# Encoder layer on eight cores: the mixer's output projection in seven products instead of eight, with casts, statistics and first loads re-queued

## The reference

```python
h = rms_norm(x, g_mix)
q, k, v, cu, cb, cc, gl = split(h @ w_in)        # 8 q heads, 2 k/v heads of 128; conv width 1024
y_attn = windowed_gqa_sink(rope(q), rope(k), v, sink) @ w_attn_out
y_conv = (cb * short_conv_centred(cc * cu, conv_w)) @ w_conv_out
g_a, g_c = split(sigmoid(gl + b_gate))
x = x + (g_a * y_attn + g_c * y_conv) @ w_o      # the output projection of this case
x = x + memory_cross_attention(rms_norm(x, g_cross), rms_norm(mem, g_mem), w_cq, w_ckv, w_co)
hf = rms_norm(x, g_ffn)
x = x + (silu(hf @ w_gate) * (hf @ w_up)) @ w_down
return rms_norm(x, g_final)
```

## Time and profile before

| | |
|---|---|
| median of 3 runs | 3403.1 us (3401.38 to 3403.25) |
| the profiled execution | 3398.95 us |
| its span (slowest core, 2) | 3397.9 us; all cores 3389.7 to 3397.9 us |
| TensorE busy | 3264.5 us (96%) |
| VectorE, ScalarE, GpSimd busy | 1916.3, 927.4, 858.1 us |
| DMA | 315.34 MB |
| granted TensorE clock, mean | 0.991 |
| chain that ended last | 90% TensorE, 4% VectorE, 2% issue |

### The profile page before, as it was taken

The page is one execution under the profiler, slowest core; times in us unless marked ns, Lnnn a source line. Parts: engine busy times, 40 slices in busy tenths (PEclk is TensorE's granted clock), DMA queues, the critical chain, the costliest instruction groups (busy, mean ns, idle before and its releaser), DMA issues.

```text
span 3397.9 us, 48543 instructions; the slowest of 8 cores (3389.7 to 3397.9 us)
## 1 busy us (share of the span) xinstructions
PE 3264.5 (96%) x15813; PEld 1534.5 (45%) x16118; DVE 1916.3 (56%) x3109; ACT 927.4 (27%) x1790; POOL 858.1 (25%) x1001
## 2 busy tenths in 40 slices
PE   5899999999899999999999999999989999999997
PEld 3455444444344444444454444444434444444445
DVE  4855644526755454635687655553386454554465
ACT  4355221135411010101453532112361011111115
POOL 1311122221222231312463112222221222222233
PEclk8999999999999999999999999999999999999999
DMA  8434544573346555545685335557333545454545
GB/s 203 77 69 75 87 82 87 91 164 56 62 70 99 75 86 87 83 80 91 132 184 118 62 56 92 85 85 177 64 60 60 90 76 96 69 98 74 96 73 139
DMA packets 117029, 315.34 MB, mean 93 GB/s; under 512 B 13488, under 2 KB 22064, under 8 KB 116784
## 3 DMA queue, kind: packets, MB, share of 16 engines
q0 software_dynamic: 81216, 256.02, 45.8%
q1 hardware_dynamic: 35568, 56.19, 5.8%
HBM read 551.36 MB, written 16.78 MB: 167 GB/s over the span
## 4 chain that ended last, share of the span: by engine, by line
PE 90%; DVE 4%; issue 2%; ACT 1%; DMA 1%; POOL 0%; SPq 0%; DVEq 0%; ACTq 0%; POOLq 0%
PE ps L333 89%; DVE arena L351 3%; ACT arena L348 1%; PE ps L336 1%; DMA arena<-xT 1%; POOL arena L351 0%; SPq L374 0%; DMA arena<-wp 0%; DVE arena L355 0%; DVE arena L362 0%; DVE arena L359 0%; DVEq L144 0%; DVE arena L368 0%; ACTq L144 0%; ACT ps L348 0%
## 5 line engine op out<-in xcount | busy, mean ns | idle before, releaser
L333 PE MATMUL ps<-arena 128*128 128x512 bf16 (+2 forms) x15317 | 3241.8, 370 | 120.7 <-DVE arena L351 53.4
L333 PEld LDWEIGHTS ps<-arena 128*128 128x128 bf16 x15622 | 1505.7, 98 | 1840.8 <-issue 166.2
L351 DVE TENSOR_TENSOR arena<-ps,arena 128x512 f32<-128x512 f32 (+4 forms) x1542 | 982.2, 660 | 1271.2 <-PE ps L333 1231.2
L348 ACT ACTIVATE arena<-arena 128x512 f32<-128x512 f32 (+8 forms) x1128 | 646.9, 620 | 1045.2 <-DVE arena L351 437.1
L351 DVE TENSOR_TENSOR arena<-arena 128x1024 bf16<-128x1024 bf16 (+5 forms) x1192 | 755.4, 669 | 125.4 <-ACT arena L348 56.3
L351 POOL TENSOR_TENSOR arena<-arena 128x512 f32<-128x512 f32 (+2 forms) x433 | 556.9, 1294 | 959.5 <-DVE arena L351 792.9
L374 POOL DMA_DIRECT2D arena<-wp x560 | 303.9, 544 | 1572.7 <-PE ps L333 1361.4
L348 ACT ACTIVATE arena<-ps 128x512 f32<-128x512 f32 (+3 forms) x332 | 212.5, 654 | 1234.1 <-PE ps L333 925.3
L348 ACT ACTIVATE arena<-ps,arena 128x256 f32<-128x256 f32 (+4 forms) x123 | 61.4, 516 | 124.6 <-PE ps L333 93.4
L359 DVE SCALAR_TENSOR_TENSOR arena<-arena 128x1024 f32<-128x1024 f32 (+1 forms) x48 | 67.8, 1428 | 23.5 <-ACT arena L348 21.6
L355 DVE TENSOR_SCALAR arena<-arena 128x4 f32<-128x4 f32 (+3 forms) x145 | 44.5, 341 | 33.5 <-DMA arena<-xT 26.7
(11 more groups left out here) (8 smaller groups left out, 6.1 us busy)
## 6 DMA issues: line engine op xcount, KB each, us to landing
arena<-wp POOLq DMA_DIRECT2D x400, 512.0 KB, 5.7
arena<-xT SPq DMA_DIRECT2D x128, 256.0 KB, 13.8
arena<-wp POOLq DMA_DIRECT2D x96, 256.0 KB, 4.2
arena<-wp POOLq DMA_DIRECT2D x64, 320.0 KB, 5.4
outT<-arena SPq DMA_DIRECT2D x48, 256.0 KB, 4.1
outT<-arena SPq DMA_DIRECT2D x32, 128.0 KB, 3.0
arena<-cs SPq DMA_DIRECT2D x4, 576.0 KB, 10.8
arena<-memT SPq DMA_DIRECT2D x16, 128.0 KB, 8.7
```

The lines of the kernel that those rows point to most:

```text
L333: pr.add("pe", lambda e: e.matmul(out, lhsT, rhs, start=start, stop=stop), reads=[lhsT, rhs], writes=[out])
L348: pr.add("act", lambda e: e.activation(out, in_, func, **kw), reads=rd, writes=wr)
L351: pr.add(eng, lambda e: e.tensor_tensor(out, in0, in1, op), reads=[in0, in1], writes=[out])
```

## The change

Six edits:

1. `out_proj` goes in pairs of weight pieces, 7 products of 8 matmuls each for 2 column chunks x 2 halves. The products are added to x in place: c1 is copied by ScalarE, u and e1 are made by VectorE, three sums (x21+u, x12+e1, x22+e1) by GpSimd, five by VectorE. Half 0's statistics are all on VectorE, half 1's all on GpSimd, with a ring of two slots. Only half 0 is cast here.
2. Token sums of `mT` (`merged_sums`, `outT`) are made in the second half of `mix`, the last behind `gated(15)`, and `pair_sums` of the first pair ahead of it.
3. Half 1 is cast in `cross`, steps t = 2 and 3.
4. `post` is split: casts first, squares and their adds later; the four banks `bs` are taken one by one; the merges for two `finish` calls are emitted earlier, and in `first_blocks` `finish` itself one block earlier.
5. `qkv_first`: V's weight loads wait for chunks 7 and 11 of x instead of 9 and 13, the cos and sin tables are loaded in the middle of the second half of x, `k_ropes(0)` comes behind all casts, and two q projections stand ahead of the halo's `finish`.
6. The 32 final chunks of tile 0: VectorE's half of them read 1/rms from a bank.

```diff
@@ generate
+    outT = chunks8([kv_lo, kv_lo + 4352, kv_lo + 6400, kv_lo + 10240, kv_lo + 14848, q_lo + 32768, c_lo + 8192, rstd_lo]
+                   + [rstd_lo + 1024 * i for i in (1, 2, 3)] + [acc_lo + 2048, acc_lo + 3072]
+                   + [h_lo + 16384 + 1024 * i for i in (8, 9, 10)] + [h_lo + 16384 + 1024 * i for i in range(8)])
+    accO = view(h_lo + 16384 + 11264, F32, (2, HW))
@@ qkv_first
-        wissue(xT[:, 0, 9, :]); wissue(xT[:, 0, 13, :])
-        load_cs(0, xT[:, 0, 13, :])
+        wissue(xT[:, 0, 7, :]); wissue(xT[:, 0, 11, :])
         for c in range(16):
             dma_x(xT[:, 1, c, :], c, HW, HW)
+            if c == 9:
+                load_cs(0)
...
-        casts(0, 6)
+        casts(0, 12)
         half_scales(0, st0)
-        casts(6, 11)
+        v_out(vb)
+        casts(12, 16)
+        ring.flush()
         k_ropes(bk, 0)
-        v_out(vb)
-        casts(11, 16)
-        ring.flush()
...
-        b = proj2(wF(("in", 0)), hk)
-        wfree()
+        qb = []
+        for h in range(2):
+            qb.append(proj2(wF(("in", h)), hk))
+            wfree()
+            for hf in range(2):
+                q_rope(qb[h][hf], h, hf)
         finish([accH], rstdH, 128)
@@ mix
-            g = gated_products(c)
-            gated(g)
-            g = gated_products(c + 1)
-            if c + 2 < 16:
-                pw = pair_load(("in", 38 + c), ("in", 39 + c))
-                pair_sums(pw)
-            gated(g)
+            for cc in (c, c + 1):
+                g = gated_products(cc)
+                if cc == c + 1 and cc < 15:
+                    pw = pair_load(("in", 37 + cc), ("in", 38 + cc))
+                    pair_sums(pw)
+                if cc == 15:
+                    pw = pair_load(("o", 0), ("o", 1))
+                    pair_sums(pw)
+                gated(g)
+                if 8 <= cc < 13:
+                    merged_sums(cc - 8)
+                elif cc == 14:
+                    merged_sums(5)
+                    merged_sums(6)
+                elif cc == 15:
+                    merged_sums(7)
+        for k in range(8):
+            tt(outT[2][k], mTs[0][8 + k], outT[1][k], ALU.subtract)
+        return pw
+
+    def merged_sums(k):
+        tt(outT[0][k], mTs[1][k], mTs[0][k], ALU.subtract)
+        tt(outT[1][k], mTs[1][8 + k], outT[0][k], ALU.subtract)
+        tt(mTs[1][k], mTs[1][8 + k], mTs[1][k], ALU.subtract)
@@ out_proj
-        sts = stat_pair(SQ4)
-        for c in range(16):
-            b = proj2(wF(("o", c)), lambda hf: lambda k: mT[:, hf, k, :])
+        ring = Squares([sq2[:, 0, :], sq2[:, 1, :]])
+        sts = [Stat({"dve": accB[:, hf, :], "pool": accO[:, hf, :]}, ring) for hf in range(2)]
...
+            def done(x, cc, hf):
+                if hf == 0:
+                    cast(hT[:, 0, cc, :], x, 1, cc, "act")
+                sts[hf].add(x, "pool" if hf else "dve")
+
+            b = part(w0[:, 0:8, :], mTs[0][0:8])
+            act(c1, bank(b), AF.Copy)
+            plus(x11, b)
+            b = part(s2, t2)
+            tt(u, bank(b), c1, ALU.add)
+            bfree(b)
+            tt(x21, x21, u, ALU.add, "pool")
+            b = part(s1, t1)
+            tt(e1, bank(b), u, ALU.add)
+            bfree(b)
+            tt(x12, x12, e1, ALU.add, "pool")
+            tt(x22, x22, e1, ALU.add, "pool")
+            b = part(w1[:, 0:8, :], mTs[1][0:8])
+            plus(x21, b, False)
+            plus(x22, b)
+            b = part(w0[:, 8:16, :], mTs[0][8:16])
             wfree()
-            for hf in range(2):
-                x = resid(b[hf], c, hf)
-                cast(hT[:, hf, c, :], x, 1, c, "act")
-                sts[hf].add(x, "dve" if c % 2 else "pool")
+            plus(x11, b)
+            if c + 2 < 16:
+                nxt = pair_load(("o", c + 2), ("o", c + 3))
+                pair_sums(nxt)
+            done(x11, c, 0)
+            done(x22, c + 1, 1)
+            b = part(s4, mTs[1][8:16])
+            plus(x12, b)
+            done(x12, c, 1)
+            b = part(w1[:, 8:16, :], t4)
+            wfree()
+            plus(x21, b)
+            done(x21, c + 1, 0)
@@ cross
+            if t in (2, 3):
+                for c in range(8 * (t - 2), 8 * (t - 1)):
+                    cast(hT[:, 1, c, :], xT[:, 1, c, :], 1, c, "dve" if c % 2 else "act")
...
-                post(2 if t < 10 else 3)
+                post_casts(2 if t < 10 else 3)
+                if t < 11:
+                    post_sums()
         co(0, 14, 2)
-        bs = [balloc() for _ in range(4)]
-        post(16)
-        new[0].ring.flush()
+        post_casts(16)
+        bs = []
+        a0 = None
         for q in range(4):
             co(1, 4 * q, 4)
-            post(4)
+            post_casts(4)
+            post_sums()
+            if q == 0:
+                new[0].ring.flush()
+            if q == 1:
+                a0 = merge(new[0].accs())
             ws = ffn_weight(q)
+            bs.append(balloc())
             for k in range(16):
                 mm(bank(bs[q]), ws[:, k, :], hT[:, 0, k, :], k == 0, k == 15)
             if q == 2:
-                finish(new[0].accs(), rstd[:, 0, :])
-        post(32)
+                finish(a0, rstd[:, 0, :])
@@ ffn, first_blocks
             s0 = [gate_half(bs0[2 * j], 0) for j in range(2)]
+            a1 = merge(sts[1].accs())
             bs1 = []
             for q in range(4):
                 bs1.append(proj(ffn_ws[q], hk(1)))
@@
                 if q == 1:
+                    finish(a1, rstd[:, 1, :])
                     for j in range(2):
                         up_scaled(s0[j], bs0[2 * j + 1], j, 0)
-                if q == 2:
-                    finish(sts[1].accs(), rstd[:, 1, :])
@@ ffn, end of tile 0
+                        held.append(balloc())
+                        finish(fst[hf].accs(), finr[:, hf, :], also=bank(held[hf]))
...
+                    final_chunk(it, hf, c, finr[:, hf, :] if i % 2 else bank(held[hf]), i % 2)
+                    if c == 14:
+                        bfree(held[hf])
```

45 lines of the change are left out of this document (31 added, 14 removed).

## The result

The kernel after takes 3369.7 us as the median of its runs against 3403.2 us before: 0.9899 of the time, with an interval of [0.9879, 0.9918]. Faster by 33 us (1.0%), where 54.5 us were forecast. The profiled execution takes 3370.68 us (span 3369.6) against 3398.95 us, which is 28.3 us less.

A forecast was written before the change was run, and what follows sets the result against it. The prediction took TensorE as the bound, busy 3264.5 of 3397.9 us. Its terms summed to -54.5 us, 3344.5 against the profiled 3398.95; carrying 4.15 to the median gave 3348.6 us, range 3322 to 3378.

The forecast's parts named there:

- Seam: Between `mix` and `out_proj`: TensorE waits 3.9 us per tile for t2[7] behind VectorE's longer queue; +7.8 us.
- Pair loop: New `out_proj`: VectorE needs 13.2 us per pair, including one SBUF meeting with GpSimd, against TensorE's 12.08; +13.2 us.
- Last chunk of hT: End of `out_proj`: VectorE is behind, so the chunk cast after product 7 is 0.8 us late for `cross`.
- Cross post and start of ffn: End of `cross`, first `ffn` blocks: new order and earlier merges remove waits and lower clock; -13.4 and -19.8 us.
- Start phase: Before `mix`: VectorE's casts ahead of `k_ropes(0)`, -6 us; both q projections ahead of the halo's `finish`, -8.5 us.
- Finals in tile 1: Tile 1's attention: final operations reading one input from a bank spare VectorE 15.6 us, shortening TensorE's waits; -4 us.
- (1): Pair loop of `out_proj` stays under 12.08 us, GpSimd's adds always missing VectorE's; 3339 us, chance 0.22.
- (2): Pair loop of `out_proj` has two VectorE-GpSimd meetings per pair, period 14.6 us; 3366 us, chance 0.12.
- (3): Start phase bound by DMA alone: the 6 us don't come, q's weights some 5 late; 3360 us, chance 0.09.
- (4): New order in `cross` makes ScalarE the bound: half of 15.4 us returns, casts at upper bound; 3361 us, chance 0.09.
- (5): Slower: VectorE and GpSimd take turns throughout `out_proj`, period 20.1 us or more; about 3454 us, chance 0.03.
- (6): The product in `out_proj` falls back behind an unseen wait of its buffers; about no change, 3403 us, chance 0.03.

The follow-up runs named there:

- experiment 1: Kernel after with the old output projection: no seven products, no merged sums, no casts in `cross`; 0.9835 of before, spans 3350.8 to 3357.9 us.
- experiment 3: Kernel after with the cast and square of x21 emitted behind the next pair's copy of c1; 0.9815 of before, span 3347.6 us.
- experiment 9: Kernel after with the old order in `cross`: `post` unsplit, four banks taken together, merges and `finish` in old places; 0.9986 of before, span 3397.6 us.
- experiment 10: Kernel after with the start phase's second q projection back behind the halo's `finish`; 0.9931 of before, span 3376.6 us.
- experiment 12: Kernel after with VectorE's sixteen final operations reading both inputs from SBUF again, no bank held; 0.9900 of before, span 3370.4 us.
- combo: Kernel after with c1's copy ahead of x21's cast and square, a shorter VectorE queue at the seam, last pair's casts before squares; ratio 0.9882, span 3345.2 us.

## Why the prediction was right in direction and 21 us too good

- **Matmuls, -27.6.** They went. Strassen's scheme still cost more than it brought: with its stage in the sum, `out_proj` and its seam were forecast at -8.2 us with the merge, and measured at +7.4 (experiment 1). This is 15.6 of the 24.5 us by which the table's sums differ.
- **Seam, +7.8.** TensorE waited 3.37 us in tile 0 where 3.9 were worked out. The term is right; a stretch of lower clock behind it was not in it. 161 matmuls took 36.59 us where 12.25 for 56 would give 35.2: 1.4 us.
- **Pair loop, +13.2.** The period was 13.9 us where 13.2 were forecast, nearly right for a wrong reason. The 11.8 us of work and of waits for GpSimd are in the rows: 0.72 and 1.76 us of waiting, 2.5 together. (The sum has 2.7, though its own figures, 3.75 less 1.2, give 2.55.) 11.8 + 1.99 is 13.8. The 1.4 us for a meeting of VectorE and GpSimd in SBUF never came in the loop: all sums take 0.68 us. The failed step is the sentence that calls ScalarE hidden because its 4.3 us of work fit into the pair. It asked how much ScalarE does, not who waits behind its queue: VectorE waited 1.99 us in each pair for the copy (experiment 3). TensorE lost 1.04 + 1.61 + 1.92 + 1.58 + 2.29 = 8.4 us in tile 0 instead of 5.8.
- **Last chunk of hT, 0.8.** TensorE waited 2.65 us for it, and 0.71 behind it for the statistics; then came 6.96 us for 21 matmuls that take 5.63 at full clock. That is core 1. On six of the eight cores the wait is 0.96 to 1.00 us in tile 0, because the row ahead of it already ran slower (15.44 us where core 1 has 13.76); in tile 1 all eight wait 2.68 us. It is the same backlog, once more ahead of `cross`.
- **Rule on SBUF.** The Trainium skill (SBUF — State Buffer, Who interferes with whom) makes such pairs of instructions exclude each other. In the pair loop of the kernel after the two queues don't meet: GpSimd's additions ran from 698.42 to 701.5 and from 702.97 to 706.7 us, VectorE's four weight sums from 708.00 to 711.7, behind them, and in the traces of all eight cores VectorE's additions with both inputs in SBUF meet one of GpSimd's only in the last pair of a tile, twice. One of the two was longer, by 0.2 us:

```profile
783.43 0.89 DVE L356 TENSOR_TENSOR arena<-arena 128x512 f32<-128x512 f32 x1 [1.44 <-ACT arena L353]
```

  GpSimd's addition at 782.48 ended 0.33 us behind its start. The 2.07 us of the earlier trace rows come again with the old output projection (experiment 1, 2.06 to 2.08 us on every core). What the traces have agrees with the rule; the forecast's error was to let the two queues meet once in every pair.
- **Merge ahead of cross, -1.6.** It can't be told apart from the waits around it.
- **Casts in cross, +5.4.** They cost 3.3 us (1.4 and 1.9, experiment 1), inside the bounds. The waits came where they were named, at P_(4): 1.47 us at 802.64.
- **Cross post and start of ffn, -33.2 together.** Measured: -31.2 (experiment 9). Mechanism and size are right; what is late next was 1.60 + 1.35 us, with 1.5 us a tile kept for it. The 1.35 us are a wait on ScalarE where 2.02 us on VectorE stood, a small form of what the prediction named as a sign of being wrong.
- **Start phase.** The second step, -8.5, was -6.9 (experiment 10), with the mechanism right. The first step, -6, was -3.3: the kernel of experiment 10 has it alone and reaches A at 133.6 us where before has 136.8. Its row of matmuls behind the last late cast did start 5.0 us earlier (middle 58.6 against 63.6), but only part of that was left at A; where the rest went is open. In the kernel after GpSimd issued behind x's last chunk at 54.7 us (middle; 54.51 on core 1), 1.5 us later than before, and TensorE waited 4.14 us on core 1 for the first late cast. The change is not the cause of the later x: with the same first loads the issue comes at 53.4 in experiment 1 and 53.5 in experiment 10, against 53.2 before. It differs from execution to execution. The clock was low behind this wait, 0.65 from 60 to 68 us, as it was before (0.61 from 63 to 71).
- **Finals in tile 1, -4.** Measured: -0.3 to -1.2 (experiment 12), towards the lower bound of 0 and inside the scatter. The term took half of the waits in the neighbourhood for the finals' doing; waits of 1.45 and 1.90 us stand there after the 15.6 us have gone from VectorE. It was also read on one core: the wait of 1.86 us at 1804.68 stands on cores 2 and 4 of the kernel before and on none of the six others.
- **The carry of 4.15 us.** The median of after lies 0.9 us under its profiled execution, not 4.15 above. This made 5 us of the 33 and came from no step: luck.

Of the rivals, (1) didn't come, since the period wasn't under 12.08; (2), a period of 14.6 by two meetings, gives a time (3366) near the measured one by a mechanism that didn't occur. (3) came in part: the first step gave 3.3 us instead of 6, but no weights of q were late by 5. (4), ScalarE as the bound in `cross`, didn't come. ScalarE mattered one stage earlier, and by its order. (5) and (6) didn't come: the period is far from 17.6 us, and the matmuls went.

A version that is better than both: combo, 3346 to 3347 us, 23 us under the kernel after. There the scheme brings 6.4 us in tile 0 and 6.8 in tile 1 over the old `out_proj` ahead of `cross`, and costs 3.3 in it. Experiment 3 alone, a few lines, gets most of that.

## What to carry to other kernels

An engine with little work can still be the one that everybody waits for: for each wait that a change adds, list what stands in the releasing engine's queue ahead of the releasing instruction and when its inputs are there, not how busy the engine is. Two readers of one PSUM bank on different engines are a chain if the program orders them; keep the first one's queue short (1.14 us a pair here), and if it can't be, put the one that is free first (0.65 us). A loop has its period from the longest chain of waits around it, and saving a wait ahead of such a loop mostly moves it inside. Read a wait on all cores before a change is built on it: the one at 1804.68 was on two of eight.
